# Root before reciprocal: the order of scale, root and reciprocal in the eight RMS norms of a one-core transformer kernel

## The reference, cut to what matters

```python
def rms_norm(x, g):
    xf = x.astype(jnp.float32)
    y = xf * lax.rsqrt(jnp.mean(xf * xf, axis=-1, keepdims=True) + EPS)
    return (y * g.astype(jnp.float32)).astype(x.dtype)
```

## Time and profile before

| | |
|---|---|
| median of 3 runs | 2049.94 us (2047.15 to 2049.99) |
| the profiled execution's own time | 2039.93 us |
| its span, first to last instruction | 2037.9 us |
| its mean granted TensorE clock | 0.943 of full speed |
| PE, DVE, ACT busy | 1889.6, 1424.0, 874.7 us |
| the eight norms' L507, L508, L497 | 424, 1753, 416 ns each |

### The profile page before, as it was taken

One profiled execution on the slowest core, in us unless ns is written; L12 is line 12 of the kernel. 1 busy time (PEld: TensorE's weight loads), 2 busy tenths in 40 slices (PEclk: granted clock), 3 DMA queues, 4 the chain that ended last, 5 costly groups with the idle time before them and its releaser, 6 DMA issues.

```text
span 2037.9 us, 41749 instructions
## 1 busy us (share of the span) xinstructions
PE 1889.6 (93%) x15336; PEld 1833.0 (90%) x15336; DVE 1424.0 (70%) x2437; ACT 874.7 (43%) x1317; POOL 19.3 (1%) x38
## 2 busy tenths in 40 slices
PE   7979997999799969997789979999999999999997
PEld 7969996988799959986679979999999999999997
DVE  5668886844688863447766549996888889994554
ACT  4333443443343335365444444455444344444443
POOL 0000000010000000000100000000000000000000
PEclk9989997976899989987999989999999999999999
DMA  5525553420455524430026624455444445554553
GB/s 199 185 98 183 181 181 100 156 93 12 164 185 185 182 87 144 135 114 1 1 83 202 200 95 145 165 165 185 166 165 166 164 150 168 167 165 167 176 176 109
DMA packets 80276, 293.70 MB, mean 144 GB/s; under 512 B 8960, under 2 KB 9120, under 8 KB 79824
## 3 DMA queue, kind: packets, MB, share of 16 engines
q1 hardware_dynamic: 79632, 289.96, 43.2%
q0 software_dynamic: 576, 2.79, 0.4%
HBM read 291.67 MB, written 1.05 MB: 144 GB/s over the span
## 4 chain that ended last, share of the span: by engine, by line
PE 81%; DVE 14%; ACT 3%; issue 2%; DMA 0%; DVEq 0%; ACTq 0%
PE ps L421 23%; PE ps L422 22%; PE ps L423 22%; DVE m L395 3%; PE ps L427 3%; PE ps L462 2%; PE ps L1492 1%; DVE m L1394 1%; DVE m L514 1%; PE ps L752 1%; DVE m L1390 1%; ACT m L383 1%; PE ps L751 1%; DVE m L1398 1%; DVE m L508 1%
## 5 line engine op out<-in xcount | busy, mean ns | idle before, releaser
L421 PE MATMUL ps<-m,m 128*128 128x256 f32 x4336 | 1252.7, 289 | 69.2 <-DVE m L522 33.8
L422 PE MATMUL ps<-m,m 128*128 128x256 f32 x4336 | 1235.0, 285 | 0.0
L423 PE MATMUL ps<-m,m 128*128 128x256 f32 x4336 | 1234.4, 285 | 0.0
L395 DVE TENSOR_TENSOR m<-m,m 128x1024 fp32r<-128x1024 f32 x546 | 663.1, 1222 | 432.1 <-ACT m L383 430.5
L421 PEld LDWEIGHTS ps<-m,m 128*128 128x128 f32 x4336 | 840.5, 194 | 83.6 <-issue 53.1
L422 PEld LDWEIGHTS ps<-m,m 128*128 128x128 f32 x4336 | 840.8, 194 | 0.6 <-issue 0.2
L423 PEld LDWEIGHTS ps<-m,m 128*128 128x128 f32 x4336 | 840.0, 194 | 0.0
L383 ACT ACTIVATE m<-m 128x1024 fp32r<-128x1024 f32 x546 | 576.1, 1056 | 472.5 <-PE ps L423 471.1
L1531 ACT ACTIVATE m<-ps 128x256 f32 (+1 forms) x128 | 49.2, 384 | 198.6 <-PE ps L423 198.5
L427 PEld LDWEIGHTS ps<-m,m 128*128 128x128 f32 (+1 forms) x412 | 64.3, 232 | 31.2 <-issue 11.4
L427 PE MATMUL ps<-m,m 128*128 128x128 f32 (+1 forms) x412 | 74.8, 338 | 14.1 <-ACT m L877 10.8
(11 more groups left out here) (198 smaller groups left out, 1131.2 us busy)
## 6 DMA issues: line engine op xcount, KB each, us to landing
m<-stream SPq DMA_DIRECT2D x546, 512.0 KB, 3.3
m<-alibi_t POOLq DMA_DIRECT2D x1, 1536.0 KB, 9.6
m<-con SPq DMA_DIRECT2D x1, 1353.0 KB, 10.1
m<-xT SPq DMA_DIRECT2D x1, 1024.0 KB, 4.9
y<-m SPq DMA_DIRECT2D x4, 256.0 KB, 2.4
m<-wcmpk POOLq DMA_DIRECT2D x1, 512.0 KB, 4.1
m<-wcmpv POOLq DMA_DIRECT2D x1, 512.0 KB, 4.8
m<-par SPq DMA_DIRECT2D x1, 178.0 KB, 5.4
```

Source lines behind the costliest of these rows:

```text
L395: nc.vector.tensor_tensor(w_lo[:, r, :], raw[:, r, :], w_hi[:, r, :].bitcast(F32), ALU.subtract)\
L421: nc.tensor.matmul(out, lhs[0], rhs[0], start=start, stop=False, **kw)
L422: nc.tensor.matmul(out, lhs[0], rhs[1], start=False, stop=False, **kw)
L423: return nc.tensor.matmul(out, lhs[1], rhs[0], start=False, stop=stop, **kw)
```

## The change

The addition of EPS and the division by D move into the activation: ACT reads the sums from PSUM and takes the root of sum/D + EPS, with 1/D as a constant scale and EPS as a bias that it reads from a new buffer `eps` of one number per partition. DVE then takes the reciprocal. The DVE instruction for scale and addition is gone, and so are two semaphores, for which one new one stands. POOL fills `eps` ahead of `ones`. The buffers behind `ones` move by eight numbers, 32 bytes, each.

```diff
-    ones = l_.take(T)
+    ones, eps = l_.take(T), l_.take(1)
...
-    recip_ready = sem("recip_ready")
-    rstd_ready = sem("rstd_ready")
+    rms_ready = sem("rms_ready")
...
-        act.wait_ge(recip_ready, n + 1)
-        nc.scalar.activation(rstd[:, :], norm_t[:, :], ACT.Sqrt).then_inc(rstd_ready, 1)
+        act.wait_ge(sum_ready, n + 1)
+        nc.scalar.activation(norm_t[:, :], ps[:, 7, 0:T], ACT.Sqrt, bias=eps[:, 0:1], scale=1.0 / D).then_inc(rms_ready, 1)
...
-        dve.wait_ge(sum_ready, n + 1)
-        dc.link(nc.vector.tensor_scalar(norm_t[:, :], ps[:, 7, 0:T], 1.0 / D, EPS, ALU.mult, ALU.add))
-        nc.vector.reciprocal(norm_t[:, :], norm_t[:, :]).then_inc(recip_ready, 1)
-        dve.wait_ge(rstd_ready, n + 1)
+        dve.wait_ge(rms_ready, n + 1)
+        dc.link(nc.vector.reciprocal(rstd[:, :], norm_t[:, :]))
...
+            nc.gpsimd.memset(eps, EPS).then_inc(s_ones, 1)
             nc.gpsimd.memset(ones[:, :], 1.0).then_inc(s_ones, 1)
...
-            pe.wait_ge(s_ones, 1)
+            pe.wait_ge(s_ones, 2)
```

## The result

| | before | the change |
|---|---|---|
| median, 5 runs each in turn | 2049.15 us (2046.64 to 2049.99) | 2060.27 us (2059.74 to 2062.15) |
| profiled execution: own time, span | 2039.93, 2037.9 us | 2061.91, 2059.9 us |
| granted clock in it | 0.943 | 0.932 |

The change made the kernel slower: the medians lie 11 us apart, and the ratio is 1.006, with a 95% interval of 1.0045 to 1.0074. The profiled execution of before was one of its quickest, so the two profiles lie 22 us apart.

The account below looks back on a forecast made before the run. PE was busy 93% of the span, but each norm was bound by a serial chain; 0.46 us removed less 0.044 us for a longer root, over eight norms, gave 2049.94 - 3.4 = 2046.5 us, range 2042.6 to 2050.4 us.

Parts of the forecast that it names:

- The removed instruction, the order and the hand-overs: In each norm, dropping DVE's scale saves 0.46 us; the reciprocal keeps 1753 ns and the remaining hand-overs pair up.
- The root in its new form: ACT's root from PSUM with a bias pointer takes 460 ns, bounds 384 and 492, using L806's exponential for the bias.
- The sum: Each norm saves 0.42 us; eight norms save 3.3 to 3.4 us, bounds 3.1 and 3.9 us.
- rivals (2): ACT's table load before the root starts only after the sums: six loads add 7.7 us, 2054.2 us; chance 0.03.
- (3): ACT is held 1.28 us after the root's table load, taking back 1.1 us: 2047.6 us; chance 0.04.
- The thin cover in norm 0: PE's sums still hide ACT's table load in norm 0, with 0.6 us of cover; costed at nothing.
- After that nothing else is due: Time cut between the sums and L514 comes off the total once per norm, with no later wait taking it back.
- rival (1): Clock behind the norms falls otherwise: three norms changing gain or lose 3.9 us, 2042.6 or 2050.4 us; no single chance given.
- The last sign that the prediction gave: Over 4 us moved with 2.28 us in every norm means the clock, with changed 0.50 stretches behind the norms.
- The shift by 32 bytes ... I cost it at nothing.: Moving buffers costs nothing, since every second gated tile of the expert stage already stood 32 bytes off the other.
- The range: 2042.6 to 2050.4 us, the two ends of the clock cases behind the norms; some 0.15 left outside.
- a clock that costs more than 7 us: An outcome in which the granted clock makes the kernel over 7 us slower; chance 0.03.

Follow-up runs that it names:

- e3: The changed kernel with one more linked DVE instruction behind each reciprocal, so each norm takes about its old time; 2040.74 us, ratio 0.9970.
- e5: The changed kernel run once more, unaltered; 2063.61 us, ratio 1.0091.
- e14: The kernel before with eight unused numbers per partition behind `ones`, so later buffers move by 32 bytes; 2040.37 us, ratio 0.9962.
- e1: The changed kernel with the new order only in norms 0 to 5, old order in 6 and 7; 2069.58 us, ratio 1.0111.
- e6: The changed kernel with PE waiting for two added DVE instructions before the nsa heads; 2068.88 us, ratio 1.0105.
- e7: The changed kernel with three idle multiplications in PE's pause at the start of the nsa heads; 2036.60 us, ratio 0.9949.
- e8: The changed kernel with three idle multiplications at the start of the nsa heads and eight at that of the moba heads; 2013.64 us, ratio 0.9832.
- e9: The changed kernel with the new order only in norms 3 to 5, old order elsewhere, buffers moved; 2072.97 us, ratio 1.0117.
- e13: The kernel before, unaltered, run again for another profile; 2046.98 us, ratio 1.0006.

## Why the prediction was wrong, point by point

- *The removed instruction, the order and the hand-overs.* Right. The path from the sums crosses as it was counted, the reciprocal kept its 1753 ns, and one hand-over to ACT costs what one to DVE did.
- *The root in its new form.* 473 ns, within the bounds of 384 and 492, above the 460 taken. Against the 384 ns of an activation that reads PSUM without a pointer, the bias costs 89 ns. The Trainium skill, "ScalarE: Activation LUTs", section "What ACT_TABLE_LOAD costs", has about 93 ns for it; the page was nearer than the row of L806.
- *The sum.* Forecast 0.42 us per norm. Measured, from the end of the sums to the first multiplication of L514: 0.41 us less in seven norms (2.74 to 2.33 us, in norm 5 2.81 to 2.40), and 0.02 us less in norm 0 (2.81 to 2.79). That is 2.9 us instead of 3.4; the longer root takes 8 x 0.013 = 0.1 of the difference, and norm 0 the rest.
- *The table load, rivals (2) and (3).* It starts at the end of the squares (in norm 0, of the last split), and there is no tail. The thin cover in norm 0 did give way, which the prediction had named but put at nothing. The root started where the load ended (timeline of the changed kernel), while the sums had ended at 11.70 + 0.81 = 12.51:

```profile
11.64 1.28 ACT L496 ACT_TABLE_LOAD   x1
12.93 0.47 ACT L496 ACTIVATE m<-ps,m 128x256 f32<-128x256 f32 x1
...
11.70 0.81 PE L461 MATMUL ps<-m,m 128*128 128x256 f32 x3
```

- *"After that nothing else is due."* This is the step that failed, and with it the pricing of rival (1). What was due was the clock of a later stage: the nsa heads took 66 us at a mean granted clock of 0.53 instead of 39 us at 1.00. The prediction looked at the clock only behind the norms, where a stretch more or less at the lower level costs 1.3 us and the next change of the clock ends it. It took from the earlier trace rows that flips are small and have no preferred sign. The page's row of the granted clock, shows slices 9 and 10 at 7 and 6 in the kernel before: that is the moba stage, 61.4 us at the lower level, and nobody asked why the nsa heads, nearly the same code, did not do the same. (Moba has one pause more, of 1.19 us, in which PE waits for a copy by POOL.) There the lower level, once taken, stayed for 61.4 us or more and cost 27 us, twenty times what was priced. The shortening also had a preferred sign, in 11 of 11 runs of the changed kernel, and padded back to the old length (e3) in none of 6. In its first profile the pause had come to stand where the clock fell; in that of e5 the clock was down before the stage. The last sign that the prediction gave, more than 4 us with the forecast length in every norm, did point to the clock, but to the stretches behind the norms.
- *"The shift by 32 bytes ... I cost it at nothing."* Wrong too: e14 is 7.8 us faster, of which 3.8 us lie in the expert stage. The argument was that both placings occur in the kernel before. But the two tiles already had different paces there (120 and 117 ns from pass to pass, which nobody had looked up), and at its new place the second has a third one, 113 ns.
- *The range.* It held the bounds of each term and was 8 us wide, but its cases were all small. The case that came, a stage at the other level, was in the trace and not among them. The prediction gave 0.03 to a clock that costs more than 7 us.

What stays open: what in the nsa and moba heads lets the lower level last for 61.4 us and more, though the profile shows PE busy nearly all the time; why the clock is down before the nsa heads begin in some profiles (e1, e5, e6, e7, e8, e9), which is how e9 and 2 of the 11 runs of the changed kernel (2074.79 and 2075.09 us) seem to get slow; why the same pause did no harm where the clock had risen 1.7 us ahead; and why passes that read a tile 32 bytes further on start 113 instead of 117 ns apart.

## What to carry to other kernels

In this kernel a change that saved a microsecond or so on the chain moved all that followed against the changes of TensorE's clock. Before it is priced, look for stages in which the granted clock is at its lower level over tens of microseconds, and for others of the same form that are not: those can flip, and their difference is the risk. A pause of PE at the start of such a stage, here 0.75 us, can be filled with a few idle multiplications. In the kernel before, filling the pauses of both stages took the time from 2048.14 to 2022.47 us, 1.4% less (ratio 0.985 to 0.9878), over seven times the 3.4 us forecast for the change; there it was the moba heads that gained, since the nsa heads had the full clock already. With the change and the moved buffers besides it brought 2011.11 us, 1.8% less (0.9808 to 0.9833).

## What the runs showed of the hardware that I had not expected

- The granted clock stayed at 0.50 for 61 to 68 us of a stage in which the profile shows PE busy without a gap (e6: 67.70 of 67.70 us, though weight loads were busy for only 56.58). With three extra multiplications at its start it rose to 1.00 in e7 and e8.
- Three extra multiplications (1.4 us of work at the full clock) at the start of a stage were worth 27 us in the changed kernel (e5 to e7), and eight in 1.9 us of pauses of the other one another 23 us (e7 to e8).
- Buffers 32 bytes further on let PE do 645 instead of 636 passes in the same 62 us (e13, e14), with the granted clock at 1.00 in both: passes that read the moved tile start 113 instead of 117 ns apart.
- An activation whose bias is a pointer takes 473 ns for 128x256 from PSUM (the changed kernel), against 384 ns without (before, L1531).
